# A mixture-of-experts encoder layer on one core: rows gathered two experts ahead, prompt products placed piece by piece

## The chip, the core and the metric

The kernel runs on one core of a Trainium2 chip. The core has TensorE (matmuls, and the loads of their stationary operand), VectorE (DVE), ScalarE (ACT), GpSimd (POOL) and SyncE (SP), each with its own queue of instructions and in step with the others through semaphores only, and 16 DMA engines that move data between HBM and on-chip memory. The metric is the device time of one execution in microseconds (us); less is better.

## What is computed

One encoder layer is applied to two groups of tokens that share the weights: the prompt (256 tokens) and the sample (1024 tokens), each token 1024 wide, all in f32. The first half of the layer is a token mixer (retention and a gated recurrence). The second half, where the change is, is a mixture of 16 experts, in which each expert chooses its tokens:

```python
def expert_choice_ffn(h, w_router, w_gate, w_up, w_down):
    bsz, s, d = h.shape
    t = h.reshape(bsz * s, d)
    n_tok = bsz * s
    cap = CAPACITY_FACTOR * n_tok // N_EXPERTS      # 128 (sample), 32 (prompt)
    aff = jax.nn.softmax((t @ w_router).astype(jnp.float32), axis=-1)
    gate, idx = lax.top_k(aff.T, cap)
    xe = t[idx]
    a = jnp.einsum('ecd,edf->ecf', xe, w_gate)      # d 1024, f 2048
    u = jnp.einsum('ecd,edf->ecf', xe, w_up)
    ye = jnp.einsum('ecf,efd->ecd', jax.nn.silu(a) * u, w_down)
    ye = ye * gate[..., None].astype(ye.dtype)
    out = jnp.zeros_like(t).at[idx.reshape(-1)].add(ye.reshape(-1, d))
    return out.reshape(bsz, s, d)
...
    x = x + ga2 * rms_norm(expert_choice_ffn(h2, w_router, w_gate, w_up, w_down), g_post2)
```

## The kernel before

The program is a row of phases. The change touches the last two, `phase_experts` and `phase_output`.

**Experts and blocks.** Expert `e` has four blocks of 512 hidden columns (`FB_N` is 4), so there are 64 blocks (`NBLK`). A block needs six weight pieces of 1 MB: four of gate and up together ("gu", two of the eight 128-row slices each) and two of down ("d"). SP loads the pieces in the order of `PIECES_W` into a ring of ten slots (`RAW`): in iteration `b` the four gu pieces of block `b`, then the two d pieces of block `b - 1`. Piece `s` goes into the slot of piece `s - 10`, and so waits until that piece was split (`s_low`) and until the prompt's products that read it are done: `s_pg` for gu and `s_pd` for d, each counted up once in a block, after the last product.

**Split of the weights.** The sample's 128 rows are multiplied with weights split in two fp32r halves, in a second ring of four slots (`SPLIT`): ACT writes the high half (`high`, L1857), DVE the rest (`low`, L1908), and TensorE does three products for each slice (L1771 to L1776 for gate and up, L1827 to L1829 for down). A slot is free again when TensorE's last matmul on the piece is done (`s_used`).

**Prompt.** The prompt's 32 rows are multiplied in plain f32, straight from the raw ring: matmuls whose stationary operand is 32 columns wide, four side by side in the array (`tile_position=(0, 32 * j)`). `gate_up_prompt` (L1796) does all four gu pieces of a block at once, `down_prompt` (L1808) both d pieces.

**TensorE's order in iteration `b`**: gate and up of pieces 0 and 1; `turn_hidden(b - 1)`, the transposes of the hidden values of the block before (into `ps_eh`, and the prompt's into columns 256 to 383 of `ps_ep`); in three iterations of four one round of `turn_x`, transposes of the gathered rows of the next expert (L1753, L1755; into `ps_ex`); gate and up of pieces 2 and 3; `gate_up_prompt(b)`; `down_prompt(b - 1)`; down of block `b - 1`. The rounds of `turn_x` for expert `e + 1` are in iterations `4e + 1`, `4e + 2` and `4e + 3`.

**ACT and DVE** go through lists written in the same way. In iteration `b` DVE does `low` of the two d pieces, `hidden_low` (the copy L1912 of the prompt's transposed hidden values, then L1914), `x_rows` and `x_low` if there is a round, `low` of the next block's gu piece 0, the product `hid_s` L1962, `low` of piece 1, the product `hid_p` L1967, and `low` of pieces 2 and 3. After an expert's last block ACT and DVE scale its results into `out_s` and `out_p`.

**POOL** issues the indirect DMAs. `gather(e)` fetches the rows of expert `e` into `rows_s` and `rows_p`, of which there is one each, so it waits for the last round of `turn_x` of expert `e - 1` (`s_xt`). The loop over `e` does `gather(e + 1)`, waits for the results of expert `e`, adds them to `moe_dram` with two indirect DMAs, and waits until these have landed before it goes on. `take_waits` is a tiny addition on POOL (`tick`, L1711) that takes the waits ahead of a DMA.

**Output.** `phase_output` goes over ten tiles of 128 tokens: ACT sums squares and takes the root, DVE scales (L2030), POOL adds the residual (L2037), SP stores the tile.

Of the kernel before, what the change touches and what calls it, by code (L numbers as in the profile page):

```python
# [13 lines left out]
ALU = mybir.AluOpType  # L14
# [3 lines left out]
P = 128  # L18
D = 1024
KC = D // P  # L20
SEQS = (256, 1024)
NTOK = sum(SEQS)
NT = NTOK // P
# [10 lines left out]
NE = 16  # L34
# [5 lines left out]
FB_N = DE // 512  # L40
# [1611 lines left out]
def phase_experts(nc, t):  # L1652
# [5 lines left out]
    with ExitStack() as ctx:  # L1658
# [27 lines left out]
        def x_round(b):  # L1686

            return b // FB_N + 1, b % FB_N - 1

        def has_x(b):  # L1690
            return b < NBLK and b % FB_N >= 1 and b // FB_N + 1 < NE
# [3 lines left out]
        @block.sync  # L1695
        def _(sp):
            sp.dma_start(t.gate2[:], t.gates_dram[1].unsqueeze(0).to_broadcast([P, 2, D])).then_inc(s_last, 16)
            for s in range(RAW, NPW):
                kind, b, i = PIECES_W[s - RAW]
                sp.wait_ge(s_low, s - RAW + 1)  # L1700
                sp.wait_ge(s_pg if kind == "gu" else s_pd, b + 1)
                load_piece(sp, t, s)
            sp.wait_ge(s_pg, NBLK)
            sp.dma_start(t.x1_sb, t.x1_dram.rearrange("(t p) d -> p t d", p=P)).then_inc(s_last, 16)
            sp.wait_ge(s_last, 32)

        @block.gpsimd
        def _(pool):
            def take_waits():

                pool.tensor_tensor(tick[:, 1:2], tick[:, 0:1], tick[:, 0:1], ALU.add)  # L1711
                pool.drain()

            def gather(e):
                if e >= 1:
                    pool.wait_ge(s_xt, 3 * e)
                    take_waits()
                for rows, idx in ((rows_s, t.idx_s), (rows_p, t.idx_p)):
                    pool.indirect_dma_start(out=rows[:], out_offset=None, in_=t.xn_dram,
                                            in_offset=bass.IndirectOffsetOnAxis(ap=idx[:, e:e + 1], axis=0)).then_inc(s_rows, 16)  # L1720

            pool.memset(tick[:], 0.0)
            pool.drain()
            gather(0)
            for e in range(NE):
                if e + 1 < NE:
                    gather(e + 1)
                pool.wait_ge(s_oact, e + 1)
                pool.wait_ge(s_oprompt, e + 1)
                pool.wait_ge(s_odve, e + 1)  # L1730
                take_waits()
                pool.indirect_dma_start(out=t.moe_dram, out_offset=bass.IndirectOffsetOnAxis(ap=t.idx_s[:, e:e + 1], axis=0),
                                        in_=out_s[:], in_offset=None, compute_op=ALU.add).then_inc(s_add, 16)
                pool.indirect_dma_start(out=t.moe_dram.rearrange("n (q d) -> (n q) d", q=4),
                                        out_offset=bass.IndirectOffsetOnAxis(ap=t.idx_q[:, e:e + 1], axis=0),
                                        in_=out_p[:], in_offset=None, compute_op=ALU.add).then_inc(s_add, 16)
                pool.wait_ge(s_add, 32 * (e + 1))
                take_waits()
                pool.sem_inc(s_stored, 1)

        @block.tensor
        def _(pe):
# [36 lines left out]
            def turn_hidden(b):  # L1779
                pe.wait_ge(s_hid, b + 1)  # L1780
                pe.wait_ge(s_hidp, b + 1)
                for k in range(4):
                    pe.transpose(ps_h[:, k * P:(k + 1) * P], hid_s[:, k * P:(k + 1) * P], t.ident[:])
                pe.transpose(ps_p[:, 256:256 + P], hid_p[:], t.ident[:]).then_inc(s_ht, 1)

            def gate_up_prompt(b):
                e = b // FB_N
                if b % FB_N == 0:
                    pe.wait_ge(s_xev, 3 * (e + 1))
                if b >= 1:  # L1790
                    pe.wait_ge(s_htp, b)
                for c in range(KC):
                    s = first_gu[b] + c // 2
                    w = t.ring[:, s % RAW].rearrange("p (m c f) -> p m c f", m=2, c=2)
                    for j in range(4):
                        mm = pe.matmul(ps_p[32 * j:32 * j + 32, 0:256], xp[:, e % 2, c], w[:, :, c % 2, j * P:(j + 1) * P],  # L1796
                                       start=(c == 0), stop=(c == KC - 1), tile_position=(0, 32 * j))
                mm.then_inc(s_pg, 1)

            def down_prompt(b):  # L1800
                pe.wait_ge(s_htp, b + 1)
                pe.wait_ge(s_low, first_d[b] + 2)
                if b % FB_N == 0 and b >= FB_N:
                    pe.wait_ge(s_oprompt, b // FB_N)
                for k in range(4):
                    w = t.ring[:, (first_d[b] + k // 2) % RAW, (k % 2) * 1024:(k % 2 + 1) * 1024]
                    for j in range(4):
                        mm = pe.matmul(ps_yp[32 * j:32 * j + 32, 0:256], hT_p[:, k], w[:, j * 256:(j + 1) * 256],  # L1808
                                       start=(b % FB_N == 0 and k == 0), stop=(b % FB_N == FB_N - 1 and k == 3),
                                       tile_position=(0, 32 * j))  # L1810
                mm.then_inc(s_pd, 1)
# [21 lines left out]
                turn_x(0, r)  # L1833
            for b in range(NBLK + 1):
                if b < NBLK:
                    gate_up(b, 0)
                    gate_up(b, 1)
                if b >= 1:
                    turn_hidden(b - 1)
                if has_x(b):  # L1840
                    turn_x(*x_round(b))
                if b < NBLK:
                    gate_up(b, 2)
                    gate_up(b, 3)
                    gate_up_prompt(b)
                if b >= 1:
                    down_prompt(b - 1)
                    down(b - 1, 0)
                    down(b - 1, 1)

        @block.scalar
        def _(act):
# [27 lines left out]
            for b in range(NBLK + 1):  # L1880
                if b >= 1:
                    high(first_d[b - 1])
                    high(first_d[b - 1] + 1)
                    hidden_high(b - 1)
                if has_x(b):
                    x_high(*x_round(b))
                if b + 1 < NBLK:
                    high(first_gu[b + 1])
                if b < NBLK:
                    act.wait_ge(s_used, first_gu[b] + 4)  # L1890
                    act.activation(silu_s[:], ps_g[:], ACT.Silu).then_inc(s_silu, 1)
                if b + 1 < NBLK:
                    high(first_gu[b + 1] + 1)
                if b < NBLK:
                    act.wait_ge(s_pg, b + 1)
                    act.activation(silu_p[:], ps_p[:, 0:P], ACT.Silu).then_inc(s_silup, 1)
                if b + 1 < NBLK:
                    high(first_gu[b + 1] + 2)
                if b >= 1 and b % FB_N == 0:
                    out(b // FB_N - 1)  # L1900
                if b + 1 < NBLK:
                    high(first_gu[b + 1] + 3)

        @block.vector
        def _(dve):
# [3 lines left out]

            def hidden_low(b):  # L1910
                dve.wait_ge(s_ht, b + 1)
                dve.tensor_copy(hT_p[:], ps_p[:, 256:256 + P].rearrange("p (k n) -> p k n", k=4)).then_inc(s_htp, 1)  # L1912
                dve.wait_ge(s_hth, b + 1)
                dve.tensor_tensor(hT_low[:], ps_h[:].rearrange("p (k n) -> p k n", k=4), hT_high[:], ALU.subtract).then_inc(s_htl, 1)  # L1914

# [17 lines left out]
                                      ALU.subtract).then_inc(s_xl, 1)  # L1933

            def out(e):
                dve.wait_ge(s_pd, FB_N * (e + 1))
                if e >= 1:
                    dve.wait_ge(s_stored, e)
                dve.tensor_scalar(out_p[:], ps_yp[:, 0:256], t.gate_q[:, e:e + 1], None, ALU.mult).then_inc(s_oprompt, 1)
                dve.wait_ge(s_used, first_d[FB_N * e + FB_N - 1] + 2)  # L1940
                dve.tensor_scalar(out_s[:, 512:D], ps_y[1][:], t.gate_s[:, e:e + 1], None, ALU.mult).then_inc(s_odve, 1)  # L1941
# [34 lines left out]
def phase_output(nc, t):  # L1976

    with ExitStack() as ctx:  # L1978
# [38 lines left out]
        def _(dve):  # L2017
            def variance(tl):
# [3 lines left out]
                dve.drain()  # L2022
                dve.reciprocal(v, v).then_inc(s_var, 1)  # L2023

            variance(0)
            for tl in range(NT):
                if tl + 1 < NT:
# [1 line left out]
                dve.wait_ge(s_std, tl + 1)  # L2029
                dve.scalar_tensor_tensor(out=moe[:, tl], in0=moe[:, tl], scalar=ss[:, tl:tl + 1],  # L2030
                                         in1=gate[:, TILE_GROUP[tl]], op0=ALU.mult, op1=ALU.mult).then_inc(s_moe, 1)

        @block.gpsimd
        def _(pool):
            for tl in range(NT):
                pool.wait_ge(s_moe, tl + 1)
                pool.tensor_tensor(x1[:, tl], x1[:, tl], moe[:, tl], ALU.add).then_inc(s_y, 1)  # L2037


class Tensors:  # L2040
# [88 lines left out]
```

## Time and profile before

| | us |
|---|---|
| median of 3 runs | 3444.46 (3437.57 to 3444.84) |
| the profiled execution | 3441.23 |
| its span in the trace | 3439.4 |
| expert phase in it: first gate matmul to last down matmul | 1653.0 to 3382.0 |

The span is from the first to the last instruction of the program in the trace, and the execution's own time lies 1.8 us above it. The profile gives for each engine how long it was busy, what it waited for, and its instructions in order of time. TensorE's busy time counts overlapping matmuls as they stand, so spacings between starts tell more than durations.

### The profile page before, as it was taken

To read this page: it belongs to the slowest core of one execution; us is meant where nothing else is said; L and a number is where in the kernel's file an instruction comes from. 1 tells how busy PE (TensorE), PEld (TensorE's weight loads), DVE (VectorE), ACT (ScalarE), POOL (GpSimd) and SP (SyncE) were. 2 spreads that over 40 slices of the span, in tenths; PEclk is the share of its full clock that TensorE was granted. 3 is DMA by queue.
4 is the path that set the end of the run, shared out by engine and by line. 5 is a ranking of instruction groups with operands and counts; after the bars stand their busy time and mean duration, and the time that the engine had idled before them with its cause. 6 is when DMAs were issued, how large, how long until landed. Compare 5 with 4: busy or idle time off the path is not lost. (4 is left out here: it accounts for less than half of the span.)

```text
span 3439.4 us, 43951 instructions
## 1 busy us (share of the span) xinstructions
PE 2946.2 (86%) x17902; PEld 2127.2 (62%) x17902; DVE 1779.8 (52%) x2181; ACT 1265.8 (37%) x1386; POOL 344.0 (10%) x262
## 2 busy tenths in 40 slices
PE   8989888998897999994888977898878988898793
PEld 3466555665666885583666766676666766676672
DVE  2166164263464102355656655565556665665565
ACT  2132132232223210142545544454444544454452
POOL 2110110110200001110011011100111011100103
PEclk9999998999998999996889989999989998999896
DMA  9201002002006225434567666676767666686685
GB/s 328 97 1 47 27 1 74 1 1 74 1 1 190 95 70 165 150 111 174 192 228 270 232 230 236 236 277 227 242 223 267 235 232 227 234 289 230 227 280 208
DMA packets 317449, 569.73 MB, mean 166 GB/s; under 512 B 24442, under 2 KB 126730, under 8 KB 316994
## 3 DMA queue, kind: packets, MB, share of 16 engines
q1 hardware_dynamic: 309572, 546.00, 45.8%
q0 software_dynamic: 7680, 20.98, 2.6%
q8 instruction: 140, 2.29, 0.3%
q14 instruction: 57, 0.47, 0.0%
HBM read 519.62 MB, written 47.28 MB: 165 GB/s over the span
## 5 line engine op out<-in xcount | busy, mean ns | idle before, releaser
L1908 DVE TENSOR_TENSOR we_low<-ring,we_high 128x2048 fp32r<-128x2048 f32 x384 | 878.1, 2291 | 443.4 <-ACT we_high L1857 443.2
L1857 ACT ACTIVATE we_high<-ring 128x2048 fp32r<-128x2048 f32 x384 | 735.9, 1918 | 510.7 <-PE ps_ey L1829 294.6
L495 PE MATMUL ps_a<-hT,w_head 128*128 128x512 f32 (+1 forms) x960 | 358.3, 533 | 31.2 <-issue 27.0
L495 PEld LDWEIGHTS ps_a<-hT,w_head 128*128 128x128 f32 x960 | 184.4, 194 | 193.8 <-issue 186.1
L1753 PE MATMUL ps_ex<-ident,rows_s 128*128 128x128 f32 x128 | 27.5, 354 | 244.0 <-DMA rows_p<-xn_dram,idx_p 242.5
L1796 PE MATMUL ps_ep<-ring,xp 128*32 128x256 f32 x4096 | 234.3, 381 | 0.0
L505 PE MATMUL ps_a<-w_head,hT 128*128 128x384 f32 x640 | 217.6, 495 | 0.0
L1771 PE MATMUL ps_eg<-we_high,xs_high 128*128 128x512 f32 x512 | 212.0, 414 | 0.3 <-DVE xs_low L1932 0.3
L1827 PE MATMUL ps_ey<-we_high,hidT_high 128*128 128x512 f32 x512 | 206.6, 403 | 0.0
L1772 PE MATMUL ps_eg<-we_low,xs_high 128*128 128x512 f32 x512 | 205.0, 400 | 0.0
L1773 PE MATMUL ps_eu<-we_high,xs_high 128*128 128x512 f32 x512 | 204.9, 400 | 0.0
L1774 PE MATMUL ps_eu<-we_low,xs_high 128*128 128x512 f32 x512 | 204.6, 400 | 0.0
L1775 PE MATMUL ps_eg<-we_high,xs_low 128*128 128x512 f32 x512 | 203.5, 398 | 0.0
L1776 PE MATMUL ps_eu<-we_high,xs_low 128*128 128x512 f32 x512 | 202.8, 396 | 0.0
L1828 PE MATMUL ps_ey<-we_low,hidT_high 128*128 128x512 f32 x512 | 200.0, 391 | 0.0
L1829 PE MATMUL ps_ey<-we_high,hidT_low 128*128 128x512 f32 x512 | 199.2, 389 | 0.0
L1711 POOL TENSOR_TENSOR tick<-tick 1x1 f32<-1x1 f32 x47 | 37.0, 787 | 1565.9 <-DVE out_s L1941 1475.7
L1796 PEld LDWEIGHTS ps_ep<-ring,xp 128*32 128x32 f32 x4096 | 126.5, 110 | 99.5 <-issue 22.5
L1753 PEld LDWEIGHTS ps_ex<-ident,rows_s 128*128 128x128 f32 x128 | 19.0, 179 | 247.9 <-DMA rows_p<-xn_dram,idx_p 245.9
L505 PEld LDWEIGHTS ps_a<-w_head,hT 128*128 128x128 f32 x640 | 121.8, 195 | 77.8 <-issue 5.0
L985 PE MATMUL ps_z<-h_high,w_high 128*128 128x512 f32 (+1 forms) x384 | 137.3, 358 | 16.1 <-DVE w_low L1039 15.6
L1216 PE MATMUL ps_g<-hT,w_br 128*128 128x512 f32 (+1 forms) x384 | 139.2, 525 | 4.0 <-DVEq L1242 4.0
(269 smaller groups left out, 4669.7 us busy)
## 6 DMA issues: line engine op xcount, KB each, us to landing
ring<-in_w_gate SPq DMA_DIRECT2D x256, 512.0 KB, 10.5
ring<-in_w_up SPq DMA_DIRECT2D x256, 512.0 KB, 11.6
ring<-in_w_down SPq DMA_DIRECT2D x256, 512.0 KB, 5.3
w_ring<-in_w_ada SPq DMA_DIRECT2D x24, 1024.0 KB, 9.7
w_head<-in_w_in SPq DMA_DIRECT2D x40, 576.0 KB, 7.6
w_z<-in_w_in SPq DMA_DIRECT2D x16, 512.0 KB, 5.2
sig_dram<-sig SPq DMA_DIRECT2D x16, 512.0 KB, 3.1
sig_g<-sig_dram SPq DMA_DIRECT2D x16, 512.0 KB, 3.9
```

Of the source, the lines that this page charges most:

```text
L495: mm = pe.matmul(bank[:, 0:m], w[:, c, g], t.hT[:, c, o:o + m], start=(c == 0), stop=(c == KC - 1))
L505: mm = pe.matmul(bank[:, 0:3 * P], t.hT[:, c, b * P:(b + 1) * P], w[:, c, QR:VR + 1], start=(c == 0), stop=(c == KC - 1))
L1771: pe.matmul(ps_g[:], xh, wg_h, start=(c == 0), stop=False)
L1772: pe.matmul(ps_g[:], xh, wg_l, start=False, stop=False)
L1773: pe.matmul(ps_u[:], xh, wu_h, start=(c == 0), stop=False)
L1774: pe.matmul(ps_u[:], xh, wu_l, start=False, stop=False)
L1775: pe.matmul(ps_g[:], xl, wg_h, start=False, stop=(c == KC - 1))
L1776: mm = pe.matmul(ps_u[:], xl, wu_h, start=False, stop=(c == KC - 1))
L1796: mm = pe.matmul(ps_p[32 * j:32 * j + 32, 0:256], xp[:, e % 2, c], w[:, :, c % 2, j * P:(j + 1) * P], start=(c == 0), stop=(c == KC - 1), ...
L1827: pe.matmul(ps_y[hf][:], hT_high[:, k], h, start=(begin and k == 0), stop=False)
L1857: act.activation(w_high[:, s % SPLIT], t.ring[:, s % RAW], ACT.Copy).then_inc(s_high, 1)
L1908: dve.tensor_tensor(w_low[:, s % SPLIT], t.ring[:, s % RAW], w_high[:, s % SPLIT], ALU.subtract).then_inc(s_low, 1)
```

## The change

Four things change, and nothing of what is computed.

- **Gather.** POOL issues `gather(0)` and `gather(1)` first, and then in the loop `gather(e + 2)` before it waits for the results of expert `e`.
- **Prompt products.** `gate_up_prompt(b, i)` and `down_prompt(b, i)` do one weight piece each, and stand right behind `gate_up(b, i)` and ahead of `down(b - 1, i)`. The transposes of the prompt's hidden values now go to `ps_ex`, so `turn_hidden` waits for the last evacuation of that bank (`s_xev`), and `turn_x`, which moves behind the third piece, waits for the copy `hidT_p` (`s_htp`). The first prompt product of a block waits for `s_hidp` in place of `s_htp`.
- **Ring slots.** `s_pg` and `s_pd` count pieces, and SP waits for the one piece that held the slot.
- **Output.** DVE adds the residual in place of POOL, one tile behind its scaling.

```diff
             for s in range(RAW, NPW):
                 kind, b, i = PIECES_W[s - RAW]
                 sp.wait_ge(s_low, s - RAW + 1)
-                sp.wait_ge(s_pg if kind == "gu" else s_pd, b + 1)
+                sp.wait_ge(s_pg if kind == "gu" else s_pd, (4 if kind == "gu" else 2) * b + i + 1)
                 load_piece(sp, t, s)
...
             gather(0)
+            gather(1)
             for e in range(NE):
-                if e + 1 < NE:
-                    gather(e + 1)
+                if e + 2 < NE:
+                    gather(e + 2)
                 pool.wait_ge(s_oact, e + 1)
...
             def turn_hidden(b):
                 pe.wait_ge(s_hid, b + 1)
                 pe.wait_ge(s_hidp, b + 1)
+                pe.wait_ge(s_xev, 3 + sum(has_x(x) for x in range(b + 1)))
...
-                pe.transpose(ps_p[:, 256:256 + P], hid_p[:], t.ident[:]).then_inc(s_ht, 1)
+                pe.transpose(ps_x[:, 0:P], hid_p[:], t.ident[:]).then_inc(s_ht, 1)
...
             for b in range(NBLK + 1):
                 if b < NBLK:
-                    gate_up(b, 0)
-                    gate_up(b, 1)
+                    for i in range(2):
+                        gate_up(b, i)
+                        gate_up_prompt(b, i)
                 if b >= 1:
                     turn_hidden(b - 1)
+                if b < NBLK:
+                    gate_up(b, 2)
+                    gate_up_prompt(b, 2)
                 if has_x(b):
+                    pe.wait_ge(s_htp, b)
                     turn_x(*x_round(b))
                 if b < NBLK:
-                    gate_up(b, 2)
                     gate_up(b, 3)
-                    gate_up_prompt(b)
+                    gate_up_prompt(b, 3)
                 if b >= 1:
-                    down_prompt(b - 1)
-                    down(b - 1, 0)
-                    down(b - 1, 1)
+                    for i in range(2):
+                        down_prompt(b - 1, i)
+                        down(b - 1, i)
...
+            def residual(tl):
+                dve.wait_ge(s_moe, tl + 1)
+                dve.tensor_tensor(x1[:, tl], x1[:, tl], moe[:, tl], ALU.add).then_inc(s_y, 1)
...
+                if tl >= 1:
+                    residual(tl - 1)
+            residual(NT - 1)
```

How the rows stand on the engines. POOL, from its first gather on, before (the name in brackets is the semaphore that the `tick` takes: `e_xt` counts rounds of `turn_x`, the three `e_o...` the results of an expert; the `tick` that stands alone follows the wait for the two DMAs into `moe_dram`):

```order
L1711 TENSOR_TENSOR tick<-tick 1x1 [waits e_xt]
L1719 DMA rows_s<-xn_dram,idx_s 128x1024
L1719 DMA rows_p<-xn_dram,idx_p 32x1024
L1711 TENSOR_TENSOR tick<-tick 1x1 [waits e_odve,e_oprompt,e_oact]
L1732 DMA moe_dram<-out_s,idx_s 1280x1024
L1734 DMA moe_dram<-out_p,idx_q 5120x256
```

The same stretch of POOL with the change:

```order
L1711 TENSOR_TENSOR tick<-tick 1x1 [waits e_xt]
L1719 DMA rows_s<-xn_dram,idx_s 128x1024
L1719 DMA rows_p<-xn_dram,idx_p 32x1024
L1711 TENSOR_TENSOR tick<-tick 1x1 [waits e_xt]
L1719 DMA rows_s<-xn_dram,idx_s 128x1024
L1719 DMA rows_p<-xn_dram,idx_p 32x1024
L1711 TENSOR_TENSOR tick<-tick 1x1 [waits e_odve,e_oprompt,e_oact]
L1733 DMA moe_dram<-out_s,idx_s 1280x1024
L1735 DMA moe_dram<-out_p,idx_q 5120x256
```

The gather of expert 2 now stands ahead of the first wait for results, and so on for every later expert.

TensorE in iteration 1, before, with the fp32r matmuls between left out (32x256 are the prompt's products, in which 8 of them belong to one weight piece):

```order
L1783 MATMUL ps_eh<-ident,hid_s 128x128 x4
L1784 MATMUL ps_ep<-ident,hid_p 128x128
L1753 MATMUL ps_ex<-ident,rows_s 128x128 x4
...
L1796 MATMUL ps_ep<-ring,xp 32x256 x32
L1808 MATMUL ps_eyp<-ring,hidT_p 32x256 x16
L1827 MATMUL ps_ey<-we_high,hidT_high 128x512
```

The same iteration of TensorE with the change, from its second weight piece on:

```order
L1777 MATMUL ps_eu<-we_high,xs_low 128x512
L1799 MATMUL ps_ep<-ring,xp 32x256 x8
L1785 MATMUL ps_eh<-ident,hid_s 128x128 x4
L1786 MATMUL ps_ex<-ident,hid_p 128x128
...
L1799 MATMUL ps_ep<-ring,xp 32x256 x8
L1754 MATMUL ps_ex<-ident,rows_s 128x128 x4
...
L1799 MATMUL ps_ep<-ring,xp 32x256 x8
L1813 MATMUL ps_eyp<-ring,hidT_p 32x256 x8
...
L1813 MATMUL ps_eyp<-ring,hidT_p 32x256 x8
```

The 32 and 16 products in one run became five runs: behind pieces 0, 1 and 2, behind piece 3 together with the first half of down, and ahead of the second half of down. The round of `turn_x` went from before piece 2 to behind it.

DVE in the output phase, for one tile in the middle, with the change (`ring` is where the residual lies; before, the last row was POOL's, L2037):

```order
L2030 TENSOR_SCALAR ss_o<-ss_o 128x1
L2032 RECIPROCAL ss_o<-ss_o 128x1
L2043 SCALAR_TENSOR_TENSOR moe<-moe,ss_o,gate 128x1024
L2036 TENSOR_TENSOR ring<-ring,moe 128x1024
```

DVE's row L2036 belongs to the tile before the one of L2043.

## Rows read from the trace of the kernel before

**Rows 1.** The page: busy time of the engines, then of 40 equal slices.
```profile
PE 2946.2 (86%) x17902; PEld 2127.2 (62%) x17902; DVE 1779.8 (52%) x2181; ACT 1265.8 (37%) x1386; POOL 344.0 (10%) x262
```
**Rows 2.** TensorE's waits from 1700 us on: us in total, times, longest.
```profile
PE ps_ex L1753 <- DMA rows_p<-xn_dram,idx_p: 232.8, 14, 17.6
```
**Rows 3.** POOL's timeline at an expert's end: start, us, instruction [idle before, releaser].
```profile
2426.15 2.07 POOL L1711 TENSOR_TENSOR tick<-tick 1x1 f32<-1x1 f32 x1 [92.70 <-DVE out_s L1941]
...
2440.09 1.00 POOL L1719 DMA_INDIRECT rows_s<-xn_dram,idx_s  x1 [0.81 <-issue]
```
**Rows 4.** TensorE's timeline at the same place.
```profile
2444.96 1.12 PE L1753 MATMUL ps_ex<-ident,rows_s 128*128 128x128 f32 x4 [15.66 <-DMA rows_p<-xn_dram,idx_p]
...
2446.73 0.63 PE L1773 MATMUL ps_eu<-we_high,xs_high 128*128 128x512 f32 x1
2447.15 0.63 PE L1774 MATMUL ps_eu<-we_low,xs_high 128*128 128x512 f32 x1
```
**Rows 5.** TensorE: first matmul of iterations 5, 30 to 33, and 61.
```profile
1760.89 0.39 PE L1771 MATMUL ps_eg<-we_high,xs_high 128*128 128x512 f32 x1
...
2463.55 0.39 PE L1771 MATMUL ps_eg<-we_high,xs_high 128*128 128x512 f32 x1
2486.43 0.39 PE L1771 MATMUL ps_eg<-we_high,xs_high 128*128 128x512 f32 x1
2509.70 0.39 PE L1771 MATMUL ps_eg<-we_high,xs_high 128*128 128x512 f32 x1
2532.14 0.39 PE L1771 MATMUL ps_eg<-we_high,xs_high 128*128 128x512 f32 x1
...
3305.96 0.39 PE L1771 MATMUL ps_eg<-we_high,xs_high 128*128 128x512 f32 x1
```
**Rows 6.** TensorE in iteration 0: into the prompt's products and out again.
```profile
1657.22 0.39 PE L1776 MATMUL ps_eu<-we_high,xs_low 128*128 128x512 f32 x1
...
1665.38 0.39 PE L1776 MATMUL ps_eu<-we_high,xs_low 128*128 128x512 f32 x1
1665.69 3.66 PE L1796 MATMUL ps_ep<-ring,xp 128*32 128x256 f32 x64
1669.29 0.50 PE L1771 MATMUL ps_eg<-we_high,xs_high 128*128 128x512 f32 x1
1669.62 0.40 PE L1772 MATMUL ps_eg<-we_low,xs_high 128*128 128x512 f32 x1
```
**Rows 7.** TensorE in iterations 28 and 30: prompt products behind prompt products, transposes behind matmuls.
```profile
2412.25 3.66 PE L1796 MATMUL ps_ep<-ring,xp 128*32 128x256 f32 x64
2415.73 1.91 PE L1808 MATMUL ps_eyp<-ring,hidT_p 128*32 128x256 f32 x32
...
2468.76 0.39 PE L1776 MATMUL ps_eu<-we_high,xs_low 128*128 128x512 f32 x1
2468.99 0.60 PE L1783 MATMUL ps_eh<-ident,hid_s 128*128 128x128 f32 x4
```
**Rows 8.** DVE's timeline in iteration 30.
```profile
2471.20 2.29 DVE L1908 TENSOR_TENSOR we_low<-ring,we_high 128x2048 fp32r<-128x2048 f32 x1 [0.42 <-ACT we_high L1857]
2473.41 0.28 DVE L1912 COPY hidT_p<-ps_ep 128x128 f32<-128x128 f32 x1
2480.37 0.68 DVE L1962 TENSOR_TENSOR hid_s<-silu_s,ps_eu 128x512 f32<-128x512 f32 x1
```
**Rows 9.** A stretch without a wait: us, busy (instructions), TensorE clock, DMA share, GB/s.
```profile
3234.00:3385.00 151.00, 147.61 (x1127) 111.34 (x1125) 97.90 (x71) 78.68 (x58) 8.57 (x6) 1.00 0.76 271
```
**Rows 10.** Timeline of the output phase.
```profile
3400.68 1.28 DVE L2030 SCALAR_TENSOR_TENSOR moe<-moe,ss_o,gate 128x1024 f32<-128x1024 f32 x1 [1.12 <-ACT ss_o L2006]
3402.22 3.27 DVE L2030 SCALAR_TENSOR_TENSOR moe<-moe,ss_o,gate 128x1024 f32<-128x1024 f32 x1
3405.56 2.35 POOL L2037 TENSOR_TENSOR ring<-ring,moe 128x1024 f32<-128x1024 f32 x1 [1.16 <-DVE moe L2030]
3430.10 5.61 POOL L2037 TENSOR_TENSOR ring<-ring,moe 128x1024 f32<-128x1024 f32 x2 [1.16 <-DVE moe L2030]
```

More of the change, by code:

```diff
@@ L1700, in _ @@
                 sp.wait_ge(s_low, s - RAW + 1)
-                sp.wait_ge(s_pg if kind == "gu" else s_pd, b + 1)
+                sp.wait_ge(s_pg if kind == "gu" else s_pd, (4 if kind == "gu" else 2) * b + i + 1)
                 load_piece(sp, t, s)
-            sp.wait_ge(s_pg, NBLK)
+            sp.wait_ge(s_pg, 4 * NBLK)
             sp.dma_start(t.x1_sb, t.x1_dram.rearrange("(t p) d -> p t d", p=P)).then_inc(s_last, 16)
@@ L1781, in turn_hidden, with gate_up_prompt @@
                 pe.wait_ge(s_hidp, b + 1)
+                pe.wait_ge(s_xev, 3 + sum(has_x(x) for x in range(b + 1)))
                 for k in range(4):
                     pe.transpose(ps_h[:, k * P:(k + 1) * P], hid_s[:, k * P:(k + 1) * P], t.ident[:])
-                pe.transpose(ps_p[:, 256:256 + P], hid_p[:], t.ident[:]).then_inc(s_ht, 1)
-            def gate_up_prompt(b):
+                pe.transpose(ps_x[:, 0:P], hid_p[:], t.ident[:]).then_inc(s_ht, 1)
+            def gate_up_prompt(b, i):
@@ L1787, in gate_up_prompt @@
                 e = b // FB_N
[L1788 to L1794, printed above, removed]
+                if i == 0:
+                    if b % FB_N == 0:
+                        pe.wait_ge(s_xev, 3 * (e + 1))
+                    if b >= 1:
+                        pe.wait_ge(s_hidp, b)
@@ L1795, in gate_up_prompt @@
+                w = t.ring[:, (first_gu[b] + i) % RAW].rearrange("p (m c f) -> p m c f", m=2, c=2)
+                for k in range(2):
+                    c = 2 * i + k
                     for j in range(4):
-                        mm = pe.matmul(ps_p[32 * j:32 * j + 32, 0:256], xp[:, e % 2, c], w[:, :, c % 2, j * P:(j + 1) * P],
+                        mm = pe.matmul(ps_p[32 * j:32 * j + 32, 0:256], xp[:, e % 2, c], w[:, :, k, j * P:(j + 1) * P],
                                        start=(c == 0), stop=(c == KC - 1), tile_position=(0, 32 * j))
@@ L1798, in gate_up_prompt, with down_prompt @@
                 mm.then_inc(s_pg, 1)
[L1800 to L1806, printed above, removed]
+            def down_prompt(b, i):
+                if i == 0:
+                    pe.wait_ge(s_htp, b + 1)
+                    if b % FB_N == 0 and b >= FB_N:
+                        pe.wait_ge(s_oprompt, b // FB_N)
+                pe.wait_ge(s_low, first_d[b] + i + 1)
+                for kl in range(2):
+                    k = 2 * i + kl
+                    w = t.ring[:, (first_d[b] + i) % RAW, kl * 1024:(kl + 1) * 1024]
@@ L1894, in _ @@
                 if b < NBLK:
-                    act.wait_ge(s_pg, b + 1)
+                    act.wait_ge(s_pg, 4 * (b + 1))
                     act.activation(silu_p[:], ps_p[:, 0:P], ACT.Silu).then_inc(s_silup, 1)
@@ L1911, in hidden_low @@
                 dve.wait_ge(s_ht, b + 1)
-                dve.tensor_copy(hT_p[:], ps_p[:, 256:256 + P].rearrange("p (k n) -> p k n", k=4)).then_inc(s_htp, 1)
+                dve.tensor_copy(hT_p[:], ps_x[:, 0:P].rearrange("p (k n) -> p k n", k=4)).then_inc(s_htp, 1)
                 dve.wait_ge(s_hth, b + 1)
@@ L1935, in out @@
             def out(e):
-                dve.wait_ge(s_pd, FB_N * (e + 1))
+                dve.wait_ge(s_pd, 2 * FB_N * (e + 1))
                 if e >= 1:
@@ L2031, in _ @@
                                          in1=gate[:, TILE_GROUP[tl]], op0=ALU.mult, op1=ALU.mult).then_inc(s_moe, 1)
[L2033 to L2037, printed above, removed]
+                if tl >= 1:
+                    residual(tl - 1)
+            residual(NT - 1)
 class Tensors:
```

## The prediction

> **What bounds the kernel now.** I read the page's busy times first: TensorE is busy for 86% of the span, no other engine for more than 52% [rows 1]. So the next view is what TensorE waited for. From 1700 us on, which is nearly the whole expert phase, there is one entry of weight: 232.8 us in 14 waits, 16.6 us each, for the gathered rows [rows 2]. The timelines say why. POOL idles for 92.70 us until the results of an expert are ready, adds them to memory, waits until they have landed, and only then issues the gather of the expert after the next, at 2440.09 [rows 3]. TensorE needs those rows one iteration into the expert and stands for 15.66 us until 2444.96 [rows 4]. The buffers had been free since three quarters of an expert earlier: it is the order in POOL's queue alone that makes the gather late.
>
> The wait has a second price. Behind it fp32r matmuls start 0.42 us apart (2446.73, 2447.15) [rows 4]; in full flow it is (1665.38 - 1657.22) / 36 = 0.227 us [rows 6]. The lower of the clock's two levels, 1.2 GHz, is granted for a while after the idle time, where the long stretch without a wait shows 1.00, that is 2.4 GHz, throughout [rows 9].
>
> Outside these waits TensorE is the bound. An iteration lasts 22.88 us with a round of the sample's rows, 23.27 with the prompt's rows, 22.45 without [rows 5].
>
> **The gather.** The 56 iterations from 5 to 60 are 14 experts' worth and hold all 14 waits: 3305.96 - 1760.89 = 1545.07 us. Without waits an expert's four iterations are 22.88 + 22.88 + 23.27 + 22.45 = 91.48 us, where the one that holds the wait is taken as its neighbour with the same instructions; 14 of them are 1280.7 us. The waits with their slow clock thus cost 1545.1 - 1280.7 = **264.4 us**, 232.8 of it idle. With the change the gather of expert e + 2 waits only for the last round of `turn_x` of expert e + 1, in iteration 4e + 3, and is needed in iteration 4e + 5. From its issue to the end of TensorE's wait it took 4.9 us (2440.09 to 2444.96), so it is more than an iteration early. What is queued behind POOL's new wait is the store of expert e; its results come in iteration 4e + 4, after that wait is over, so nothing is delayed. All 264.4 us should go, unless something else comes late.
>
> **The prompt's products in pieces.** No product is added, but TensorE goes between full-width matmuls and the 32-column ones more often. Before, each of the 65 iterations has one run of these products. With the change iteration 0 has four, iterations 1 to 63 have five (those behind gu piece 3 and the first of down adjoin), and the last has two: 4 + 315 + 2 - 65 = 256 more. The price of one trip can be read in iteration 0, where a single run stands between full-width matmuls: from the last matmul ahead to the second behind it is 1669.62 - 1665.38 = 4.24 us [rows 6]; two matmuls are 0.45, and a run of 64 records takes 3.48 where more of its kind follow (2412.25 to 2415.73) [rows 7]. That leaves 0.31 us. From a whole iteration: 22.45 - 72 x 0.227 - 1.5 x 3.48 = 0.89 us for one trip and `turn_hidden`; its five transposes, at some 0.11 us each, leave 0.34. I take 0.34, since short runs pay their start-up each: 256 x 0.34 = **87 us**, on the path, as TensorE is the bound. It is not the waits or the change of number format that cost this: the transposes in f32 start 0.23 us after a full-width fp32r matmul, like the next matmul would [rows 7]. In addition `turn_x` loses its place behind `turn_hidden` and stands between prompt products and matmuls of its own; 45 rounds at about 0.1 us are 4 us. Bounds for the trip: 0 if it came from something else, 0.45 if a short run pays another 0.1 for its start; 0 to 115 us in all.
>
> The Trainium skill speaks against this part: by its page "TensorEngine Tiling (Array Packing)", section Tiling Modes (Key Properties), changing the tiling mode drains TensorE. It gives no price there. From the page "TensorE: Matmul & The Clock Gate" (some 128 cycles of drain; a weight load of its columns over 1.2 GHz) an estimate would be two drains of 0.053 and one exposed load of 0.107, 0.21 us a trip and 55 us in all, 32 us less than by the rows. The rows decide, as they hold the whole trip.
>
> **New waits on TensorE.** `turn_x` now waits for the copy `hidT_p`, which DVE makes after it has split the second d piece, and that follows TensorE's last use of gu piece 1. In iteration 30, which starts at 2463.55, the split starts 7.65 us in and the copy at 9.86, ending at 10.14 [rows 5, 8]. With the change piece 1 ends 3.48 / 4 + 0.34 = 1.21 us later, and the copy at 11.35. TensorE comes to `turn_x` after three pieces with products and `turn_hidden`: 3 x (12 x 0.227 + 1.21) + 0.55 = 12.35 us. So 1.0 us of slack; the cover is thin, and each 0.1 us of lateness beyond it costs 4.5 us over 45 rounds. Then DVE gets the new rows at about 12.9 us instead of 10.7, and what stands behind them in its list, up to `hid_s` (16.8 us in before, [rows 8]), moves by 2.2 us to 19.0, where the next iteration, now 22.45 + 4 x 0.34 = 23.8 us long, asks for it at 23.8. The wait of `turn_hidden` for the bank is for an evacuation of the iteration before, and that of the first prompt product for `hid_p` comes 1.2 us before `turn_hidden` would ask for it anyway. I put these at nothing.
>
> **Ring slots one by one.** Slots come free earlier, and no piece was late before: no wait of TensorE for a weight stands in the list [rows 2]. Without gather waits the experts need 24 pieces of 1.05 MB in 91.48 + 16 x 0.34 = 97 us, 260 GB/s, and the stretch without waits drew 271 at a DMA share of 0.76 [rows 9]. Nothing gained, nothing lost.
>
> **Output.** The first scaling on DVE has POOL idle and takes 1.28 us, the second, beside POOL's addition, 3.27; POOL starts its two last tiles at 3430.10 and ends 5.61 us later, at 3435.7 [rows 10]. With the change a tile is on DVE alone: 1.54 us from one scaling to the next (3400.68 to 3402.22), and an addition of 128x1024, half of the split's 128x2048 at 2.29 [rows 8]: 1.15, with gaps 2.8 in all. The last addition ends at 3400.7 + 1.3 + 9 x 2.8 + 1.2 = 3428.4, **7.5 us** earlier. Bounds: were the addition as slow as POOL's 2.35, it would be 3 us later than now; 9 earlier at best.
>
> **Sum**, against the profiled execution's 3441.2: 3441.2 - 264.4 + 87 + 4 - 7.5 = 3260. The median is 3.2 us above that execution, so 3263.
>
> **Rivals.** *Cheap switches*: the array changes mode for much less than one trip shows, say 0 to 0.2 us, because in pieces the change overlaps. For it: only one place a block shows the trip. Against it: iteration 0 and the full iteration agree. 3176 to 3227 us; 9%. *A new wait*: DVE or ACT comes late by 0.5 to 1.5 us in each iteration because rows, splits and copies now chain with TensorE. For it: the thin 1.0 us. Against it: DVE is busy for 52%, with idle time in each iteration. 27 to 80 us more: 3290 to 3343; 15%. *The wait stays in part*: the gather is issued early, but lands late beside the weights' transfers or POOL meets DVE. Half of 264 us stays: 3395; 3%. That the change doesn't do what it says is ruled out by the rows on POOL, where the gather stands ahead of the wait. *Slower*: TensorE's clock. With no idle time the phase is 1.6 ms of unbroken work, and the trace has no full-level stretch of that length. If the lower level were granted in the middle of it, each matmul would take 0.42 instead of 0.227, 1.85 times as long; the gain of 181 us is gone when 181 / 0.85 = 213 us of the work, one seventh, fall to it. At a quarter (390 us) it gives 3263 + 330 = 3590. Every drop that I can see follows idle time; 2%.
>
> **How the numbers follow.** The forecast of 3263 has 70%, with 3240 to 3291 from the trip's 0.25 to 0.45 us. The range takes in half of the cheap switches and half of the new waits: 3225 to 3315, with 2 in 10 or less outside. Faster by over 0.2% (7 us, about what a measurement of this kernel can tell from no change) are all cases but the last and a piece of the third: 96%; within it 1%; slower 3%.
>
> **What would show it.** TensorE's waits for `rows_p` gone but for the first; iterations of 23.8 us without a round and the clock at 1.00 through the phase; gaps of 0.31 to 0.37 us around each run of eight products; no entry `ps_ex` waiting for `hidT_p`; the last addition on DVE some 7 us earlier against the phase's start. The prediction is wrong where iterations differ from 23.8, or where a wait stands ahead of `turn_x` or a weight piece.

## The result and the profile after

The changed kernel takes **3260.9 us** (median of 4 runs, 3258.7 to 3261.7), the kernel before 3444.4 us (median of 4, 3437.6 to 3444.8). The ratio is 0.9471, with a 95% interval of 0.9454 to 0.9487. The profiled execution took 3261.0 us, its span 3258.8.

The page's busy row, which answers to [rows 1]:

```profile
PE 3005.2 (92%) x17902; PEld 2057.2 (63%) x17902; DVE 1779.9 (55%) x2191; ACT 1256.3 (39%) x1386; POOL 326.2 (10%) x252
```

TensorE's waits from 1600 us to the end (us in total, times, longest), against [rows 2]. Left out are the waits of the phase ahead, two of 1.8 and 1.5 us in the first rounds of `turn_x`, ahead of iteration 0, and three of 0.4 us or less:

```profile
PE ps_ex L1754 <- DMA rows_p<-xn_dram,idx_p: 9.4, 1, 9.4
...
PE ps_ep L1799 <- DVE hid_p L1976: 0.6, 1, 0.6
PE ps_eg L1772 <- issue: 0.5, 1, 0.5
```

One wait for gathered rows is left, that of expert 0, ahead of the first iteration. The 14 others are gone, and from iteration 0 on no wait stands at `turn_x`. The view of stretches, over nearly all of the expert phase (us, busy of TensorE, weight loads, DVE, ACT, POOL, TensorE clock, DMA share, GB/s):

```profile
1800.00:3190.00 1390.00, 1390.00 (x10146) 949.35 (x10142) 961.47 (x712) 743.17 (x557) 135.04 (x95) 1.00 0.82 270
```

TensorE is busy for 1390.00 of 1390 us, and the clock is at its upper level, 2.4 GHz, for all of it. (What the trips between wide and narrow matmuls cost does not show in this share: it only shows in the spacings below.) POOL's timeline, against [rows 3]:

```profile
2318.67 0.18 POOL L1711 TENSOR_TENSOR tick<-tick 1x1 f32<-1x1 f32 x1 [45.76 <-PE ps_ex L1756]
2319.66 2.97 POOL L1719 DMA_INDIRECT rows_s<-xn_dram,idx_s  x1 [0.81 <-issue]
...
2355.85 0.19 POOL L1711 TENSOR_TENSOR tick<-tick 1x1 f32<-1x1 f32 x1 [32.02 <-DVE out_s L1950]
```

The gather is now released by the last round of `turn_x` (L1756) at 2318.67, 37 us before the results of the expert ahead come (2355.85). TensorE's first matmuls of iterations 5, 26 to 29 and 61, against [rows 5]:

```profile
1772.03 0.39 PE L1772 MATMUL ps_eg<-we_high,xs_high 128*128 128x512 f32 x1
2281.39 0.39 PE L1772 MATMUL ps_eg<-we_high,xs_high 128*128 128x512 f32 x1
2305.68 0.39 PE L1772 MATMUL ps_eg<-we_high,xs_high 128*128 128x512 f32 x1
2330.19 0.39 PE L1772 MATMUL ps_eg<-we_high,xs_high 128*128 128x512 f32 x1
2354.11 0.39 PE L1772 MATMUL ps_eg<-we_high,xs_high 128*128 128x512 f32 x1
3130.21 0.39 PE L1772 MATMUL ps_eg<-we_high,xs_high 128*128 128x512 f32 x1
```

An iteration takes 24.29 us with a round of the sample's rows, 24.51 with the prompt's, 23.92 without. Fourteen experts take 3130.21 - 1772.03 = 1358.2 us in place of 1545.1: 186.9 us less. One of the short runs of prompt products, against [rows 6]:

```profile
2341.10 0.39 PE L1777 MATMUL ps_eu<-we_high,xs_low 128*128 128x512 f32 x1
2341.42 1.07 PE L1799 MATMUL ps_ep<-ring,xp 128*32 128x256 f32 x16
2342.42 0.50 PE L1772 MATMUL ps_eg<-we_high,xs_high 128*128 128x512 f32 x1
2342.76 0.40 PE L1773 MATMUL ps_eg<-we_low,xs_high 128*128 128x512 f32 x1
```

From the last matmul ahead to the second behind it are 1.66 us, of which two matmuls are 0.45 and sixteen records 0.87: 0.34 us for the trip, where the run of 64 before left 0.31. With the slightly wider spacings that follow, an iteration of four trips more is 23.92 - 22.45 = 1.47 us longer, 0.37 us each on the mean.

### The profile page after: what moved, and what is told of

The parts are those of the page before. It is cut to its first block and busy times, and to the rows that moved or that the text cites. A ratio compares the mean times of both kernels' runs of the same rounds, so it can differ in the third digit from the quotient of the medians.

```text
span 3258.8 us, 43981 instructions
## 1 busy us (share of the span) xinstructions
PE 3005.2 (92%) x17902; PEld 2057.2 (63%) x17902; DVE 1779.9 (55%) x2191; ACT 1256.3 (39%) x1386; POOL 326.2 (10%) x252
## 5 line engine op out<-in xcount | busy, mean ns | idle before, releaser
L1799 PE MATMUL ps_ep<-ring,xp 128*32 128x256 f32 x4096 | 274.5, 385 | 0.6 <-DVE hid_p L1976 0.6
L1772 PE MATMUL ps_eg<-we_high,xs_high 128*128 128x512 f32 x512 | 220.1, 430 | 0.8 <-issue 0.5
L1832 PE MATMUL ps_ey<-we_high,hidT_high 128*128 128x512 f32 x512 | 215.1, 420 | 0.0
L1799 PEld LDWEIGHTS ps_ep<-ring,xp 128*32 128x32 f32 x4096 | 106.9, 109 | 135.7 <-issue 90.9
L1711 POOL TENSOR_TENSOR tick<-tick 1x1 f32<-1x1 f32 x47 | 11.5, 244 | 1386.1 <-PE ps_ex L1756 681.1
L1832 PEld LDWEIGHTS ps_ey<-we_high,hidT_high 128*128 128x128 f32 x512 | 95.8, 187 | 70.4 <-issue 51.9
L986 PE MATMUL ps_z<-h_low,w_high 128*128 128x512 f32 (+1 forms) x384 | 136.6, 356 | 0.0
```

Of the source, the lines that this page charges most:

```text
L1772: pe.matmul(ps_g[:], xh, wg_h, start=(c == 0), stop=False)
L1832: pe.matmul(ps_y[hf][:], hT_high[:, k], h, start=(begin and k == 0), stop=False)
```

## The experiments

The kernel before was run beside each of these; its medians were 3439.6, 3441.9 and 3439.0 us in the three groups. "Combined" below is the kernel of the second experiment.

### The gather alone

In the kernel before, only this:

```diff
             gather(0)
+            gather(1)
             for e in range(NE):
-                if e + 1 < NE:
-                    gather(e + 1)
+                if e + 2 < NE:
+                    gather(e + 2)
```

> The kernel before with the gather two experts ahead and nothing else. Theory (the order of POOL's queue alone made the wait, and the weights keep up with slots released by the block): the 14 waits and their slow clock go, iterations stay at 22.45 us, 3441 - 264 = 3177 us (3172 to 3185). Rival (without the waits the ring runs dry unless slots are released one by one): TensorE waits for weight pieces, iterations of over 23 us, 3210 us or more.

Measured: 3178.6 us (2 runs), ratio 0.9242 (0.9223 to 0.9261), 261 us less than before. A stretch of its trace:

```profile
1800.00:3100.00 1300.00, 1300.00 (x10060) 984.79 (x10053) 946.94 (x705) 743.09 (x553) 159.47 (x95) 1.00 0.83 289
```

TensorE never stands, its iterations are 22.45, 22.88 and 23.27 us as without a wait before, and slots released by the block feed it at 289 GB/s. The first matmuls of iterations 5 and 61:

```profile
1764.25 0.39 PE L1772 MATMUL ps_eg<-we_high,xs_high 128*128 128x512 f32 x1
3044.87 0.39 PE L1772 MATMUL ps_eg<-we_high,xs_high 128*128 128x512 f32 x1
```

The 56 iterations from 5 to 60 take 1280.62 us in place of 1545.07: 264.4 us less. The rival falls: this one edit brings the whole gain of the waits and needs nothing of the rest.

### The gather and the output

The same, and the residual on DVE as in the changed kernel's `phase_output`; prompt products and slots as before.

> The kernel before with the gather ahead and the residual added on DVE, prompt products in one run a block as before. Theory: the two gains add, 3177 - 9.7 = 3167 us (3160 to 3175), 94 us under the changed kernel, as its pieces only cost. Rival: the pieces and the single slots are what lets the gain appear, then it is not under 3240 us.

Measured: 3166.6 us (4 runs, 3166.1 to 3171.1), ratio to before 0.9211 (0.9195 to 0.9227). It beats both kernels: 94 us below the changed one. The pieces therefore only cost.

### The output alone

> The kernel before with the residual added on DVE in place of POOL. Theory (DVE's scaling ran at 3.2 us because POOL's addition stood beside it, 1.28 without): from the first scaling to the end of the last addition 26 us in place of 35, total 3441 - 9.7 = 3431 to 3435 us. Rival (the gain in that phase came from the calmer experts ahead of it): no change.

Measured: 3430.6 us (7 runs), ratio 0.9972 (0.9960 to 0.9983), 9.0 us less and half a microsecond under the expected 3431 to 3435. The timeline of its output phase, against [rows 10]:

```profile
3402.25 1.27 DVE L2034 SCALAR_TENSOR_TENSOR moe<-moe,ss_o,gate 128x1024 f32<-128x1024 f32 x1
3403.43 1.22 DVE L2027 TENSOR_TENSOR ring<-ring,moe 128x1024 f32<-128x1024 f32 x1
...
3424.44 2.35 DVE L2027 TENSOR_TENSOR ring<-ring,moe 128x1024 f32<-128x1024 f32 x2
```

The scaling that took 3.27 us beside POOL's addition takes 1.27, with the same inputs. DVE alone does both in less time than the scaling took. Which engine pays is seen in the trace of before, at the second tile and at the last:

```profile
3402.04 2.36 POOL L2037 TENSOR_TENSOR ring<-ring,moe 128x1024 f32<-128x1024 f32 x1 [10.89 <-DVE moe L2030]
...
3429.94 1.27 DVE L2030 SCALAR_TENSOR_TENSOR moe<-moe,ss_o,gate 128x1024 f32<-128x1024 f32 x1
3430.10 3.31 POOL L2037 TENSOR_TENSOR ring<-ring,moe 128x1024 f32<-128x1024 f32 x1 [1.16 <-DVE moe L2030]
```

POOL's addition at 3402.04 began ahead of the scaling at 3402.22 and kept its 2.36 us, while the scaling ended 1.1 us behind it. At the last tile DVE began first and took 1.27 us, and POOL's addition took 3.31 in place of 2.35. The second to start is the slow one, whichever engine it is. The Trainium skill has the mechanism on its page "SBUF — State Buffer", section Who interferes with whom: a DVE instruction with two inputs in SBUF contends with a GpSimd instruction that reads SBUF, and the second to start is blocked. The trace agrees: the second to start took 3.27 us in place of 1.27 on DVE, and 3.31 in place of 2.35 on POOL.

### The pieces alone

The changed kernel with `gather` and `phase_output` put back.

> The changed order of the prompt's products with slots released one by one, but gather and output as before. Theory: 256 more trips into narrow matmuls cost 89 us; in return turn_x, which waits for the gather, stands 6.3 us further back in its iteration, so each of the 14 waits shrinks from 16.6 to about 10.3 us, 88 us in all. The two cancel: 3430 to 3450 us with waits of about 145 us in the list. Rival (costs simply add): waits stay at 232 us and the time is 3530.

Measured: 3437.9 us (10 runs), ratio 0.9994 (0.9984 to 1.0003). TensorE's only wait from 1700 us on, and its end in one expert:

```profile
PE ps_ex L1753 <- issue: 138.6, 14, 10.6
...
2010.71 1.09 PE L1753 MATMUL ps_ex<-ident,rows_s 128*128 128x128 f32 x4 [10.06 <-issue]
```

(The profile names no releaser here; it is the first transpose of the gathered rows, as in [rows 4].) The waits shrank from 232.8 to 138.6 us, 6.7 us each, because the consumer of the late rows moved back in its iteration. That pays for the 256 trips almost to the microsecond. A part that costs 90 us on top of the gather shows as no change on top of the wait.

### Fewer trips

The changed kernel with its prompt products in two runs an iteration:

```diff
                 if b < NBLK:
                     for i in range(2):
                         gate_up(b, i)
+                    for i in range(2):
                         gate_up_prompt(b, i)
...
                     gate_up(b, 3)
-                    gate_up_prompt(b, 3)
+                    for i in range(2, 4):
+                        gate_up_prompt(b, i)
                 if b >= 1:
                     for i in range(2):
                         down_prompt(b - 1, i)
+                    for i in range(2):
                         down(b - 1, i)
```

(`gate_up_prompt(b, 2)` is taken out behind piece 2.)

> The changed kernel with the prompt's products in two runs an iteration (pieces 0 and 1; pieces 2 and 3 with all of down) in place of five, 192 trips fewer. Theory (each trip between full-width and narrow matmuls costs 0.37 us, whatever is in it): 3261 - 71 = 3190 us, iterations of 22.8 us. Rival (the longer iteration comes from the products' own work or from waits in the new order): no change, 3261 us.

Measured: 3190.1 us (2 runs), 71 us below the changed kernel for 192 trips: 0.37 us each. Some 2.7 us of this are an earlier start of the expert phase in this execution. The first matmuls of iterations 28 and 29:

```profile
2298.43 0.39 PE L1772 MATMUL ps_eg<-we_high,xs_high 128*128 128x512 f32 x1
...
2321.17 0.39 PE L1772 MATMUL ps_eg<-we_high,xs_high 128*128 128x512 f32 x1
```

Iterations without a round are thus 22.75 us. One run an iteration gives 22.45, two 22.75, five 23.92: 0.30 us for the second run and 0.39 for each of the other three. The price goes with the number of trips, though not quite evenly, and not with the products, of which there are as many in all three. Waits have no part in it: from 1675 us on TensorE waits 1.3 us in all.

### A visit to the narrow mode, and one in full width

Combined, with one extra f32 matmul that adds zeros in the middle of each gate and up piece, 256 in all, and no wait there. Narrow:

```diff
                     mm = pe.matmul(ps_u[:], xl, wu_h, start=False, stop=(c == KC - 1))
+                    if k == 0:
+                        pe.matmul(ps_g[0:32, 0:32], zero[:, 0:32], zero[:, 0:32], start=False, stop=False, tile_position=(0, 0))
```

and in full width `pe.matmul(ps_g[:, 0:32], zero[:], zero[:, 0:32], start=False, stop=False)`.

> The kernel with gather ahead and output on DVE, plus in each gate and up piece, in the middle of its twelve matmuls, one narrow f32 matmul of 32 columns by 32 that adds zeros; 256 visits, no wait at them. Theory (going into narrow mode and out again is what costs): 0.35 to 0.45 us a visit, 90 to 115 us over the kernel without them, 3257 to 3282 us. Rival (the price belonged to semaphore waits or to the start of a run of four side by side): its own 0.05 us, 13 us in all, about 3180.

> The same visits with a full-width f32 matmul, 128 columns by 32, that adds zeros, so that the array's mode stays. Theory (the price is the change of mode): only its own weight loads show, at most 0.25 us a visit, 3167 to 3231 us. Rival (any f32 matmul among fp32r ones breaks the flow, narrow or not): at least 0.5 us a visit, 3295 us or more.

Measured: 3274.4 us narrow and 3231.5 us in full width (2 runs each), 108 and 65 us over combined, 0.42 and 0.25 us a visit. The timelines, narrow first:

```profile
2311.92 0.39 PE L1780 MATMUL ps_eu<-we_high,xs_low 128*128 128x512 f32 x1
2312.24 0.25 PE L1782 MATMUL ps_eg<-zero 128*32 128x32 f32 x2
2312.42 0.50 PE L1775 MATMUL ps_eg<-we_high,xs_high 128*128 128x512 f32 x1
2312.75 0.39 PE L1776 MATMUL ps_eg<-we_low,xs_high 128*128 128x512 f32 x1
```

```profile
2303.15 0.40 PE L1780 MATMUL ps_eu<-we_high,xs_low 128*128 128x512 f32 x1
2303.39 0.30 PE L1782 MATMUL ps_eg<-zero 128*128 128x32 f32 x2
2303.53 0.48 PE L1775 MATMUL ps_eg<-we_high,xs_high 128*128 128x512 f32 x1
2303.84 0.39 PE L1776 MATMUL ps_eg<-we_low,xs_high 128*128 128x512 f32 x1
```

The narrow visit enters 0.32 us behind the last full-width matmul, the wide one 0.24, near the usual 0.227: going in costs 0.09 us only where the mode changes. Coming out, the first full-width matmul starts 0.18 and 0.14 us behind the visit, and the second 0.33 and 0.31 behind the first. So the slow second matmul behind a visit is not the mode's: a short wide matmul shows it too. The visit with a quarter of the stationary columns costs 0.17 us more, though its weight load is the shorter one (0.11 against 0.19 us in the traces); I put this difference down to the mode. The verdict on the mode is thus "a large part", not all: what a wide visit pays, 0.25 us, lies at the upper edge of what I had allowed (3231.5 us against at most 3231), and some of it may be in the price of a trip too; the runs do not part the two further. Semaphore waits have no part in it, as there is none at a visit.

### Slots released by the block

```diff
-                sp.wait_ge(s_pg if kind == "gu" else s_pd, (4 if kind == "gu" else 2) * b + i + 1)
+                sp.wait_ge(s_pg if kind == "gu" else s_pd, (4 if kind == "gu" else 2) * (b + 1))
```

> The changed kernel, but a slot is given back only when all prompt products of its kind in the block are done, as before the change. Theory (the ring of ten has slack either way): same time within 3 us, 3258 to 3264 us. Rival (single release carries part of the gain): slower by 20 us or more, with waits of ACT for the ring.

Measured: 3259.3 us (2 runs), against 3260.9 with single slots. Single release brings nothing here.

### A shorter ring

What single release could be worth shows when slots are scarce. In both kernels SP waits four pieces longer for each slot:

```diff
-                kind, b, i = PIECES_W[s - RAW]
-                sp.wait_ge(s_low, s - RAW + 1)
+                kind, b, i = PIECES_W[s - RAW + 4]
+                sp.wait_ge(s_low, s - RAW + 5)
```

Combined, with slots released by the block:

> Gather ahead and output on DVE, slots released by the block, and SP waits four pieces longer for each slot, so that the ring works like one of six slots. Theory (single release only pays where the ring is short): a block's first gate and up piece can be asked for only at 15 us of 22.5, lands near 20, is split at 24.5, so TensorE waits 2 to 3 us or more an iteration: 3300 to 3360 us. Rival (transfers are fast enough whatever the release): 3167 us.

The changed kernel, with single slots:

> The changed kernel with the same four pieces of extra waiting, slots released one by one. Theory: each piece is asked for at least 9 us before it is needed, no waits, 3261 us (3256 to 3270). Rival (a short ring starves this order too): 3300 us or more.

Measured: 3597.9 us and 3259.5 us (one run each). The direction is as expected and the size of the first is not: 431 us, 6.7 us an iteration, where I had 2 to 3. One iteration in its timelines, of SP, ACT and TensorE:

```profile
2306.95 0.38 SPq L1552 DMA_DIRECT2D ring<-in_w_gate  x1
...
2314.09 1.91 ACT L1858 ACTIVATE we_high<-ring 128x2048 fp32r<-128x2048 f32 x1 [9.07 <-DMA ring<-in_w_up]
...
2319.03 0.77 PE L1772 MATMUL ps_eg<-we_high,xs_high 128*128 128x512 f32 x1 [4.80 <-DVE hid_s L1963]
```

From the request to the start of the split are 7.1 us, not the 4 to 5 that I had assumed, and behind that split DVE has `hid_s` in its list, for which TensorE stands until 2319.03. There are 62 such stops, 272.5 us in all. They also bring the lower clock back: 0.90 on the mean from 1800 to 3500 us. With single slots the same short ring does nothing to the time (3259.5). So the changed kernel has slack that the other lacks: it is worth no time with ten slots, but 338 us between the two kernels with six, the trips of the second included. The two differ in two things, the release of single slots and the products placed piece by piece, without which hardly any slot could be let go earlier. The pieces with release by the block were not run with six slots, so the shares of the two are not shown.

## Why the prediction was right, point by point

Forecast 3263 us, measured 3260.9. The span of the profiled execution fell by 180.6 us (3439.4 to 3258.8):

| term | forecast | measured | from |
|---|---|---|---|
| waits for rows, with their clock | -264.4 | -264.4 | the gather alone, iterations 5 to 60 |
| 256 trips | +87 | +94 | 256 x 0.37 |
| `turn_x` apart | +4 | -5 | rounds, below |
| output phase | -7.5 | -9.7 | last `out_s` to end: 57.4, then 47.7 |
| start of the experts | 0 | +4.4 | starts 2.1 later, and iterations 0 and 1 |

The measured column makes -264.4 + 94 - 5 - 9.7 + 4.4 = -180.7. The forecast made -180.9. The waits were right for the reason given, but that the total comes so close is luck: the other four terms missed by +7, -9, -2.2 and +4.4 us and cancel.

**The waits.** This step held whole: with the gather alone the kernel takes 3178.6 us against 3177 worked out.

**The trips.** The term was read at one place in iteration 0, 0.31 us, and from a whole iteration, 0.34, and I took 0.34. Measured are 0.37: several matmuls behind a trip also start up to 0.01 us wider than usual, which the two ends of one trip don't show. Cheap switches, the first rival, fall with the experiments on two runs and on visits. Of the reason that I gave, the change of mode, the wide visit leaves only part: a short f32 matmul in full width breaks the flow for 0.25 us too. I had ruled out the number format from the way into the transposes alone [rows 7]. The way out of them, in iteration 30 before, looks different:

```profile
2469.54 0.60 PE L1753 MATMUL ps_ex<-ident,rows_s 128*128 128x128 f32 x4
2469.89 0.47 PE L1771 MATMUL ps_eg<-we_high,xs_high 128*128 128x512 f32 x1
2470.21 0.39 PE L1772 MATMUL ps_eg<-we_low,xs_high 128*128 128x512 f32 x1
```

The second fp32r matmul behind f32 transposes comes 0.32 us after the first, as behind narrow products and behind a visit. Behind a run of transposes this costs next to nothing, since the first comes early: the whole run of nine takes 0.11 us each, both ends included. So the slow second matmul goes with f32 work ahead of it, narrow or wide. How the rest of a trip parts between the mode and the number format is not shown.

**`turn_x`.** The sign was wrong. A round of the sample's rows cost 0.43 us before (22.88 - 22.45) and costs 0.37 now (24.29 - 23.92); the prompt's 0.82 and now 0.59. I charged the round 0.1 us for standing alone behind narrow products; but by the spacings the way out of the narrow mode is paid once, whatever follows. Per expert that is 0.06 + 0.06 + 0.23 = 0.35 us less, 15 times. The misses of this term and of the trips, -9 and +7, cancel.

**New waits.** DVE's timeline in iteration 26, which starts at 2281.39, against [rows 8]:

```profile
2290.30 2.29 DVE L1917 TENSOR_TENSOR we_low<-ring,we_high 128x2048 fp32r<-128x2048 f32 x1 [1.68 <-ACT we_high L1866]
2292.51 0.28 DVE L1921 COPY hidT_p<-ps_ex 128x128 f32<-128x128 f32 x1
...
2294.31 0.69 DVE L1934 TENSOR_TENSOR xs<-ps_ex,scale 128x512 f32<-128x512 f32 x1 [0.93 <-PE ps_ex L1754]
...
2300.48 0.68 DVE L1971 TENSOR_TENSOR hid_s<-silu_s,ps_eu 128x512 f32<-128x512 f32 x1
```

The copy ends 11.4 us into the iteration (forecast 11.35), the new rows reach DVE at 12.9 (12.9), and `hid_s` starts at 19.1 (19.0). TensorE's transposes started at 2293.62, 0.8 us behind the copy's end: the slack was there, and as thin as said. Two short waits did come, both once, in iteration 1: 0.5 us ahead of its first matmul, for which the profile names no releaser, and 0.6 us for `hid_p`.

**Slots.** "Nothing gained, nothing lost" held: 3259.3 with them released by the block.

**The output.** The step that missed is the spacing of the tiles: 2.6 us (the forecast had 2.8), since DVE's small instructions start while the large one ends. The addition took 1.22 us against 1.15, and even so the phase gained 2 us more. (By the forecast's own ends, 3435.7 and 3428.4, its term is 7.3, not 7.5.) Its largest part is the one named, the scaling back at 1.27 us.

**The start**, which had no term: the phase itself started 2.1 us later in this execution, and the two waits in iteration 1 make 1.1. The rest is the clock. The two stretches are from the start of iteration 0 on in after, and from 3 us behind it in before:

```profile
1655.00:1661.00 6.00, 5.93 (x20) 4.09 (x24) 5.27 (x5) 3.23 (x3) 2.90 (x3) 0.50 0.37 111
...
1656.00:1661.00 5.00, 5.00 (x22) 4.07 (x22) 3.84 (x3) 3.21 (x2) 1.04 (x1) 0.95 0.34 116
```

The lower level, 0.50, lasted for 6 us in after and for some 3 in before, where TensorE did the same work until then. The first weight piece took 0.8 us longer by it, and the run of prompt products that now stands behind it took 1.36 us to the next matmul in place of 1.00. The gather alone, without any pieces, shows the same 6 us at 0.50, so this is not the pieces' doing; what sets its length the runs do not show.

The slower rival, the clock falling in unbroken work, did not happen: the clock stands at 1.00 over the 1390 us shown above.

## What to carry to other kernels

When one engine's queue holds both a prefetch and the wait for results, put the prefetch first as soon as its buffer is free: here three lines were worth 261 us, and the prompt products in pieces gave 94 of them back. Count how often TensorE goes between full-width and narrow matmuls; at 0.37 us a trip, runs of narrow products should be as few as the ring allows, and giving buffers back earlier is worth trips only where a computing engine stands for data that could not be asked for in time (SP's own waits for slots are no sign of it: 976 us of them behind gate and up products in the changed kernel cost nothing). Measure each part on top of the part that removes the wait: the pieces alone looked free, as their cost went into a wait that would have been there anyway.

## What the runs showed that I had not expected

A single short f32 matmul in full width, 128 stationary columns by 32 moving, costs 0.25 us between fp32r matmuls, while one more transpose in a run of them costs 0.11: visits are dear even without a change of mode. And a ring shortened from ten slots to six costs 431 us where the prompt's products stand in one run and let go of their slots together, and nothing in the changed kernel: a request waits 7.1 us until its data can be used, and once TensorE stands for over 4 us an iteration, its clock falls to a mean of 0.90 and adds to the loss.
